# Last layer of a two-layer encoder trunk: embedding gate before its projection, final scale spread by products of rstd with the identity, last output tile on GpSimd

## The reference

```python
for i in range(DEPTH):                                       # DEPTH = 2
    x = x + 0.5 * swiglu(rmsnorm(x, norm_ff1[i]), ...)       # FF1
    x = x + token_mixer(rmsnorm(x, norm_mix[i]), ...)        # MIX
    x = x + 0.5 * swiglu(rmsnorm(x, norm_ff2[i]), ...)       # FF2
    g = jax.nn.sigmoid(rmsnorm(x, norm_ple[i]) @ ple_w_gate[i])
    x = x + g * (p[i] @ ple_w_proj[i])                       # PLE: 1024x1024 gate, 256x1024 projection
return rmsnorm(x, norm_final)
```

## Time and profile before

| | before |
|---|---|
| median of 3 runs | 1180.99 us |
| span of the profiled execution | 1179.5 us |
| TensorE busy | 1168.9 us (99%) |
| VectorE busy | 814.0 us (69%) |
| ScalarE busy | 593.7 us (50%) |
| GpSimd busy | 122.8 us (10%) |

### The profile page before, as it was taken

How to read it: one execution, slowest core, us unless ns; L and a number is a source line. 1 busy time by engine, 2 the same in 40 slices (tenths; PEclk the granted TensorE clock), 3 DMA queues, 4 the chain that set the end, 5 groups by cost and what they waited for, 6 DMA issues and landing times.

```text
span 1179.5 us, 24037 instructions
## 1 busy us (share of the span) xinstructions
PE 1168.9 (99%) x10534; PEld 1144.7 (97%) x10534; DVE 814.0 (69%) x939; ACT 593.7 (50%) x669; POOL 122.8 (10%) x136
## 2 busy tenths in 40 slices
PE   9999999999999999999999999999999999999997
PEld 9999999999999999999999999999899999999996
DVE  5866555688978766655786665558798777666455
ACT  5544445555745544444554444447367455444443
POOL 2000001011512000001210000100133020000011
PEclk9999999999999999999999999999999999999998
DMA  7655555545445555555555555554635365555541
GB/s 288 235 203 188 193 201 177 184 156 202 145 149 207 190 188 206 183 204 187 179 202 194 194 199 184 197 203 139 214 140 169 118 235 203 184 204 186 186 172 36
DMA packets 33384, 218.87 MB, mean 186 GB/s; under 512 B 5184, under 2 KB 6016, under 8 KB 7296
## 3 DMA queue, kind: packets, MB, share of 16 engines
q1 hardware_dynamic: 33280, 217.34, 53.2%
HBM read 216.15 MB, written 1.05 MB: 184 GB/s over the span
## 4 chain that ended last, share of the span: by engine, by line
PE 98%; DVE 1%; DMA 1%; ACT 0%; issue 0%; POOL 0%; SPq 0%; POOLq 0%; DVEq 0%
PE psum L385 31%; PE psum L387 31%; PE psum L386 31%; PE psum L665 1%; PE psum L644 1%; DMA x_all<-in_x 1%; PE psum L517 0%; PE psum L578 0%; PE psum L628 0%; PE psum L699 0%; PE psum L424 0%; PE psum L710 0%; PE psum L613 0%; DVE gates L1671 0%; PE psum L733 0%
## 5 line engine op out<-in xcount | busy, mean ns | idle before, releaser
L1222 DVE TENSOR_TENSOR w_lo<-raw,w_hi 128x2048 fp32r<-128x2048 f32 x200 | 457.9, 2293 | 213.5 <-ACT w_hi L856 213.4
L856 ACT ACTIVATE w_hi<-raw 128x2048 fp32r<-128x2048 f32 x201 | 385.2, 1917 | 366.6 <-PE psum L387 360.8
L385 PE MATMUL psum<-hA_hi,w_hi 128*128 128x256 f32 x1360 | 377.9, 278 | 0.0
L386 PE MATMUL psum<-hA_hi,w_lo 128*128 128x256 f32 x1360 | 375.7, 276 | 0.0
L387 PE MATMUL psum<-hA_lo,w_hi 128*128 128x256 f32 x1360 | 375.7, 276 | 0.0
L385 PEld LDWEIGHTS psum<-hA_hi,w_hi 128*128 128x128 f32 x1360 | 255.4, 188 | 2.7 <-issue 2.7
L386 PEld LDWEIGHTS psum<-hA_hi,w_lo 128*128 128x128 f32 x1360 | 255.4, 188 | 0.0
L387 PEld LDWEIGHTS psum<-hA_lo,w_hi 128*128 128x128 f32 x1360 | 255.3, 188 | 0.0
L385 PE MATMUL psum<-hB_hi,w_hi 128*128 128x256 f32 x832 | 230.3, 277 | 1.1 <-DVE w_lo L1654 1.1
L386 PE MATMUL psum<-hB_hi,w_lo 128*128 128x256 f32 x832 | 229.7, 276 | 0.0
L387 PE MATMUL psum<-hB_lo,w_hi 128*128 128x256 f32 x832 | 229.7, 276 | 0.0
(11 more groups left out here) (182 smaller groups left out, 1226.0 us busy)
## 6 DMA issues: line engine op xcount, KB each, us to landing
raw<-in_weights SPq DMA_DIRECT2D x203, 1024.0 KB, 4.9
raw<-in_weights SPq DMA_DIRECT2D x2, 512.0 KB, 6.2
out<-gates SPq DMA_DIRECT2D x3, 256.0 KB, 2.2
x_all<-in_x SPq DMA_DIRECT2D x1, 520.0 KB, 3.9
x_all<-in_x SPq DMA_DIRECT2D x1, 512.0 KB, 6.2
relu<-in_p SPq DMA_DIRECT2D x2, 256.0 KB, 5.0
consts<-in_consts SPq DMA_DIRECT2D x1, 384.0 KB, 5.7
out<-gates SPq DMA_DIRECT2D x2, 128.0 KB, 2.3
```

What stands on the lines that cost most here:

```text
L385: pe.matmul(o, lh, rh, start=start, stop=False)
L386: pe.matmul(o, ll, rh, start=False, stop=False)
L856: act.activation(w_hi[:, s, :], raw[:, s, :], ACT.Copy).then_inc(hi_ready[s], 1)
L1222: dve.tensor_tensor(w_lo[:, s, :], raw[:, s, :], w_hi[:, s, :].bitcast(F32), ALU.subtract).then_inc(lo_ready[s], 1)
```

## The change

In the last layer alone, the chunks of PLE are reordered in memory: four gate chunks, then the projection. TensorE follows that order (`embed_last`). The gate's four pairs are scaled by rb and put through tanh in eight tiles of `gates`; the projection then comes in five units (pairs 0, 1 and 2, tiles 6 and 7). For units 0 and 1 VectorE makes (tanh + 1) times the projection and GpSimd adds it to x; for units 2 to 4 VectorE does both. The factor 0.5 is taken into p, in both layers. In the final norm the diagonal is gone: TensorE multiplies rstd, broadcast along the free dimension, with the identity, once into bank 4 and once into bank 5. VectorE scales tiles 0 to 6 from bank 4; ScalarE copies bank 5 to SBUF, GpSimd scales tile 7 with it, and ScalarE's queue stores it. TensorE also runs 8, 2 and 8 products of ones whose results nobody reads (`idle_products`). In the first layer, adding to x takes a TENSOR_TENSOR in place of a SCALAR_TENSOR_TENSOR of the same shape.

```diff
-STORES = (slice(0, 2), slice(2, 4), slice(4, 6), slice(6, 7), slice(7, 8))
+STORES = (slice(0, 2), slice(2, 4), slice(4, 6), slice(6, 7))
+POOL_TILE = 7
+IDLE = (8, 2, 8)
+LAST_GATE_BANKS = (0, 2, 3, 4)
+LAST_UNITS = ((0, 2, 5), (2, 4, 6), (4, 6, 0), (6, 7, 1), (7, 8, 2))
...
 # TensorE
+            def embed_last(L):
+                s = operands(L, PROJ)
+                for m in range(4):
+                    pe.wait_ge(h_ready, of_norm(L, 3, m + 1))
+                    for c in range(2):
+                        mm = pairs(s, LAST_GATE_BANKS[0], hA, c, (2 * m, 2 * m + 1))
...
+                for first, stop, b in LAST_UNITS:
...
+                    mm.then_inc(unit_ready, 1)
...
+            idle_products(IDLE[0])
             pe.wait_ge(sq_added, of_norm(L_N, 0, 3) + START)
             for c in range(3):
+                if c == 2:
+                    idle_products(IDLE[1])
                 if c:
                     pe.wait_ge(last_squares, c)
...
-            spread(L_N, 0, 4)
+            idle_products(IDLE[2])
+            pe.wait_ge(rstd_done, L_N * 4 + 1)
+            for b in (4, 5):
+                for t in range(2):
+                    mm = pe.matmul(bank[b][:, t * P:(t + 1) * P], rstd[:, t:t + 1].to_broadcast([P, P]), ident, start=t == 0,
+                                   stop=True, skip_group_check=True)
+                mm.then_inc(rb_sum, 1)
...
 # ScalarE, embed_last, behind the four tanh
+                for m in range(3):
+                    if m < 2:
+                        act.wait_ge(pool_added, m + 1)
+                    else:
+                        act.wait_ge(unit_added, 1)
+                    squares(L, 4, m)
...
+                for c in range(2):
+                    act.wait_ge(unit_added, 2 + c)
+                    act.activation(last_squared[:, c, :], x[:, 6 + c, :], ACT.Square).then_inc(last_squares, 1)
...
 # GpSimd
+                if last:
+                    for m in range(2):
+                        pool.wait_ge(unit_gated, m + 1)
+                        xs = x[:, 2 * m:2 * m + 2, :]
+                        pool.tensor_tensor(xs, xs, gates[:, 2 * m:2 * m + 2, :], ALU.add).then_inc(pool_added, 1)
                 norm(L, 4, 3 if last else 4)
+                if last:
+                    pool.wait_ge(rb_ready, L_N * 4 + 1)
+                    pool.wait_ge(final_scaled, 5)
+                    last_tile = final[:, POOL_TILE, :]
+                    pool.tensor_tensor(last_tile, last_tile, rb[:, :], ALU.mult).then_inc(pool_out, 1)
...
 # VectorE, embed_last
+                for u, (first, stop, b) in enumerate(LAST_UNITS):
+                    dve.wait_ge(unit_ready, u + 1)
+                    dve.wait_ge(last_tanh, min(u, 3) + 1)
+                    g = gates[:, first:stop, :]
+                    ins = dve.scalar_tensor_tensor(out=g, in0=g, scalar=1.0, in1=tiles(b)[:, 0:stop - first, :], op0=ALU.add, op1=ALU.mult)
+                    if u < 2:
+                        ins.then_inc(unit_gated, 1)
+                    else:
+                        step(L, ins)
+                        xs = x[:, first:stop, :]
+                        dve.tensor_tensor(xs, g, xs, ALU.add).then_inc(unit_added, 1)
```

More of the change, by code:

```diff
@@ L818, in embed, with idle_products @@
                         spread(L, 3, 7)
+            def idle_products(n):
+                for _ in range(n):
+                    pe.matmul(bank[7][:, 0:P], ones[:, :], ones[:, :], start=True, stop=True)
+            def embed_last(L):
[4 more added lines that the diff above has]
+                        mm = pairs(s, LAST_GATE_BANKS[0], hA, c, (2 * m, 2 * m + 1))
+                mm.then_inc(chunk_done[s], 1)
+                token_sums(L, 3, 7)
+                for i in range(1, 4):
+                    s = operands(L, PROJ + i)
+                    by_columns(s, bank[LAST_GATE_BANKS[i]], hA).then_inc(chunk_done[s], 1)
+                    if i == 1:
+                        spread(L, 3, 7)
+                s = operands(L, PROJ + 4)
+                pe.wait_ge(p_lo, L + 1)
+                wh, wl = (w[:, s, :].rearrange("p (k n) -> p k n", n=1024) for w in (w_hi, w_lo))
+                for first, stop, b in LAST_UNITS:
+                    if b == LAST_GATE_BANKS[0]:
+                        pe.wait_ge(last_scaled, 1)
+                    if b == LAST_GATE_BANKS[1]:
+                        pe.wait_ge(last_scaled, 2)
+                    for m in range(first, stop):
+                        for k in range(2):
+                            mm = three(bank[b][:, (m - first) * T:(m - first + 1) * T], wh[:, k, m * P:(m + 1) * P],
+                                       wl[:, k, m * P:(m + 1) * P], pT_hi_[:, k, :], pT_lo_[:, k, :], k == 0, k == 1)
+                    mm.then_inc(unit_ready, 1)
             start_counts(pe, chunk_done)
@@ L1081, in embed @@
                     act.wait_ge(x_done if c else tile_added, (L * 16 + 16) if c else (L + 1))
-                    if last:
-                        act.activation(last_squared[:, c, :], x[:, 6 + c, :], ACT.Square).then_inc(last_squares, 1)
-                    else:
[L1085 to L1092, removed]
+                    act.activation(hB[0][:, 6 + c, :], x[:, 6 + c, :], ACT.Copy, scale=gains[:, 4, 6 + c:7 + c]
+                                   ).then_inc(h_hi_ready if c else tile_hi, 1)
@@ L1587, in embed @@
                     dve.tensor_tensor(gate_sum, tiles(4 + i), both(rb), ALU.mult).then_inc(pgate_scaled, 1)
-                    if i and not last:
+                    if i:
                         rest_pair(L, 4, i - 1, hB)
@@ L1592, in embed @@
                     xs = x[:, 2 * i:2 * i + 2, :]
-                    dve.scalar_tensor_tensor(out=xs, in0=gate_act, scalar=0.5, in1=xs, op0=ALU.mult, op1=ALU.add).then_inc(x_done, 1)
-                    if n + 3 == CHUNKS and not last:
+                    dve.tensor_tensor(xs, gate_act, xs, ALU.add).then_inc(x_done, 1)
+                    if n + 3 == CHUNKS:
                         split_pieces(L, n + 3)
@@ L1619, in embed, with embed_last @@
                     xs = x[:, 6 + c, :]
[L1620 to L1630, removed]
+                    dve.tensor_tensor(xs, gate_act[:, c, :], xs, ALU.add).then_inc(x_done if c else tile_added, 1)
+                rest_tile(1).then_inc(h_ready, 1)
+                dve.wait_ge(hi_ready[turn(L, PGATE + 5)[0]], turn(L, PGATE + 5)[1])
+                for i in range(4):
+                    next_piece(i)
+                split(L, PGATE + 6)
+            def embed_last(L):
+                split(L, PROJ + 3)
+                dve.wait_ge(rb_ready, L * 4 + 4)
+                for i in range(4):
+                    chunk_products(L, PROJ + i)
+                    b = LAST_GATE_BANKS[i]
+                    t = gates[:, 2 * i:2 * i + 2, :]
+                    dve.tensor_tensor(t, tiles(b) if i else high(b), both(rb), ALU.mult).then_inc(last_scaled, 1)
+                    if i == 1:
+                        split(L, PROJ + 4)
+                for u, (first, stop, b) in enumerate(LAST_UNITS):
[5 more added lines that the diff above has]
+                        ins.then_inc(unit_gated, 1)
+                    else:
+                        step(L, ins)
+                        xs = x[:, first:stop, :]
+                        dve.tensor_tensor(xs, g, xs, ALU.add).then_inc(unit_added, 1)
+                mean_square(L, 4, 4)
             start_counts(dve, lo_ready)
@@ L1636, in layer @@
                 ffn(L, FF2, 1, 3, hA)
-                embed(L, last)
-                assert steps[0] == VECTOR_STEPS, steps
+                if last:
+                    embed_last(L)
+                else:
+                    embed(L)
+                assert steps[0] == (LAST_VECTOR_STEPS if last else VECTOR_STEPS), steps
                 steps[0] = 0
@@ L1666, in _ @@
             dve.wait_ge(rb_sum, L_N * 4 + 1)
[L1667 to L1672, removed]
+            for i, m in enumerate(STORES):
+                dve.wait_ge(final_scaled, i + 1)
+                dve.tensor_tensor(final[:, m, :], final[:, m, :], bank[4][:, 0:T].unsqueeze(1).to_broadcast([P, m.stop - m.start, T]),
+                                  ALU.mult).then_inc(out_ready, 1)
 def constants():
@@ L1717, in weight_chunks @@
     mix += [columns(w["w_out"][L], 256 * i) for i in range(4)]
-    ple = [rows(w["ple_w_proj"][L], 0, 1024)] + [columns(w["ple_w_gate"][L], 256 * i) for i in range(4)]
+    proj, gate = [rows(w["ple_w_proj"][L], 0, 1024)], [columns(w["ple_w_gate"][L], 256 * i) for i in range(4)]
+    ple = gate + proj if last else proj + gate
     return [c.reshape(P, 2048) for c in ffn("ff1") + mix + ffn("ff2") + ple]
```

85 lines of the change are left out of this document (59 added, 26 removed).

## The result

The changed kernel takes 1187.66 us (median of five runs, 1186.54 to 1188.19) against 1181.03: a ratio of 1.0051, 95% interval 1.0041 to 1.0062. It is **slower by 6.6 us**, where 1187.5 was predicted. The span of the profiled execution is 1185.9 us, 6.4 over that of before.

A forecast was written before the change was run, and what follows sets the result against it. TensorE, 99% busy, bounds the kernel, with a serial tail behind it. GpSimd's later sums, then idle products and spread at the low clock, end the span at 1186.2; plus 1.49 gives 1187.7, rounded to 1187.5 us, range 1183.8 to 1189.0.

The forecast's parts named there:

- Front free: Start of the last PLE: gate first costs nothing, FF2's last pair being ready 1.4 us before TensorE needs it.
- Mean tied to GpSimd's serial chain: Final norm: serial additions and squares of pairs 0 to 2 delay the sums by 4.5 us, and the mean with them.
- The rival in which the chain does not decide: Tail: pairs' sums ready by 1169.4 as before, mean unmoved, 1180.1 us, not slower; chance 0.13.
- Sums' start: TensorE's sums of the pairs in the final norm start at 1173.85 us; 1173.1 without slowing beside VectorE.
- The upper bound, 1.90 us for each addition to x: GpSimd's additions of pairs to x at 1.90 us instead of 1.30, putting the sums at about 1174.9.
- Tile 7 ready when it was before: Last tile in the final norm: its squares reach TensorE by 1170.69 us, as before the change.
- Fall of the clock ahead of the sums: Tail: with little work for 4.7 us TensorE's clock falls to 1.2 GHz before the sums; chance of this case 0.52.
- That it would last through the spread: Second step of the fall: the low clock persists, eight idle products take 3.4 us and the spread 1.2.
- A clock of 1.0 at the spread: Sign in the new profile: full granted clock while rstd is spread would prove the low clock's lasting wrong.
- The held clock as a rival: Tail: the clock stays at 2.4 GHz through the idle products, giving 1184.6 us; chance 0.32.
- the 1186.2 of the sum: End of the span in us with the clock fallen: 6.7 us later than before, VectorE's scaling starting at 1181.2.
- Idle products, not rstd, release the spread: Final norm: the eight idle products end after rstd is ready, at 1177.4 against 1176.85 us at 2.4 GHz.

The follow-up runs named there:

- e3: e2 with a buffer of its own for the squares of each of pairs 0 to 2, idle products 16, 2, 4: 1183.18 us, ratio 1.0017 to before.
- e4: e2 with VectorE instead of GpSimd adding units 0 and 1 to x, idle products 15, 2, 4: 1183.86 us, ratio 1.0024 to before.
- e6: e5 with TensorE summing tiles 4 to 7 directly, GpSimd adding squares of pairs 0 and 1 only, idle products 4, 0, 4: 1180.96 us.
- e2: The changed kernel with 22, 2 and 4 idle products in place of 8, 2 and 8: 1184.28 us, ratio 1.0026 to before.
- b3: b2 with tile 7 also scaled on GpSimd and stored by ScalarE's queue: 1180.44 us, ratio 0.9992 to before.
- e5: The edits of e3 and e4 together, idle products 12, 2, 4: 1182.83 us, ratio 1.0014 to before.
- b2: The kernel before, old order, with the spread by rstd and identity and 4, 1, 4 products of ones: 1180.39 us, ratio 0.9992.

## Why the prediction was right

- **Front free:** right. The last dense product kept its time to 0.01 us.
- **Mean tied to GpSimd's serial chain:** right, and shown three ways: by the new trace, by e3 and e4, which shorten the chain and move the sums with it, and by e6, which takes GpSimd off it and has the mean nearly back. The rival in which the chain does not decide is out.
- **Sums' start:** predicted 1173.85, with 1173.1 if nothing slowed GpSimd; it was 1173.20. The step that was off is the direction of the slowing. GpSimd's first sum of squares started at 1167.69, 0.06 us ahead of VectorE's addition, and took its plain 0.74; VectorE took 1.22 for 0.69. In e4 GpSimd came second and took 1.21. In the rows of before VectorE had been first each time, so they could not tell. The upper bound, 1.90 us for each addition to x, rested on a wrong reading, that a long wait makes the addition slow: the first one followed a wait of 17.88 us, and the two together took 2.65. In the trace of before the three operations of about 1.90 us among that were followed up (starts at 863.94, 875.63 and 890.51) each started inside one of VectorE's splits, which read two SBUF tensors; another of this shape, behind a wait of 3.40 us but just after a split, took 1.30 (start 883.90). So 1.30 was the right choice for another reason than the one given.
- **Tile 7 ready when it was before:** wrong, at no cost. Its squares ended at 1172.15, at 1170.64 before: ScalarE takes them behind those of pair 2, which wait for GpSimd. The pairs' sum came later still, at 1173.15.
- **Fall of the clock ahead of the sums:** right; it came within 1172 to 1173. **That it would last through the spread:** wrong. A clock of 1.0 at the spread was named as the sign against this second step, and the sign came: 0.92 within 1179 to 1180, 1.00 in the us behind it.
- **The held clock as a rival:** with the clock held by other means (e2) the median was 1184.28, where that rival said 1184.6; e2 is not quite its kernel, with four products behind the sums for eight. Behind this rival stood the Trainium skill, "TensorE: Matmul & The Clock Gate", section "What's actually happening", by which the moment of a change of the clock moves from run to run. The two halves of e4's runs, one kernel at two mean clocks, agree with it.
- **Sizes:** errors both ways that nearly cancel, so that 1187.66 against 1187.5 is in part luck. The sums started 0.65 us early. At the low clock, first sum to mean took 3.6 us, not 2.8. The eight idle products held the spread for 3.1 us, not 3.4. The clock was back for the spread, so bank 4 was read 0.65 us after the spread began, not 1.3. And from the first scaling to the end it was 5.55 us, not 5.0: I had taken off 0.4 for VectorE's missing fifth operation, which b3 shows to be worth nothing. Together they leave the span 0.3 us under the 1186.2 of the sum.
- **Idle products, not rstd, release the spread:** right, by 1.9 us in the profiled execution.

The change's five runs fall into two groups, near 1186.55 and from 1187.66 to 1188.19. Spans differ likewise (1184.7 and 1184.8 against 1185.9 to 1186.4). A clock that comes back earlier in some would do that; their mean granted clocks are 0.997 in the two shorter and 0.996 or 0.997 in the three longer, which does not settle it, and the trace is of one execution only: open.

## What to carry to other kernels

An order that shortens the path behind the last product can still lengthen the tail, if it moves work that ran beside dense products behind them; count what a slower helper engine then does in series, and whether one small buffer makes it wait for another. Idle products helped here where they left at most 0.76 us without work ahead of the sums (e2 to e5, clock held in the traces) and ended before the operand that they precede; with 3.06 us left, and eight of them holding up the spread, they did harm. 22, 2, 4 were worth 3.4 us of median over 8, 2, 8, with nothing else changed. Take the parts of a bundled change apart: here the spread with a held clock gained 0.9 us in the old order, and the reordering hid it.

## What was not expected of the hardware

- Where VectorE and GpSimd each read two SBUF tensors at once in these traces, the one that started second took longer: VectorE's addition 1.22 us instead of 0.69 in the change, GpSimd's 1.21 instead of 0.74 in e4, while the first kept its own time in both.
- TensorE was busy throughout by the profile and the clock fell all the same, in the one traced execution of e6: four products of ones and then 128x1 sums up to 1171.7, busy 1.00 in each us, and the granted clock went from 2.4 to 1.2 GHz within 1171 to 1172. In b2, with four products ahead of the sums too, one between them and twelve rows of sums where e6 has twenty, it was 1.00 through the spread, as in e2. What made the difference is not shown.
